# A hybrid attention and SSD encoder layer: 44 of 48 gate and SSD-input tiles multiplied ahead of the heads, in pairs of seven block products

## The reference

```python
h = rmsnorm(x, pre_norm_g)
proj = h @ w_in                                   # 2048 x 13376
q, k, v, z_attn, z_ssm, xbc, dt_raw = split(proj)
o = dilated_attention(q, k, v, rel_bias_table)    # 16 heads x 128
attn_out = rmsnorm(o, attn_norm_g) * silu(z_attn)
ssm_out = ssd_branch(z_ssm, xbc, dt_raw, ...)     # conv 5 + silu, SSD both ways, 32 heads x 64, gate, group rmsnorm
mix = concatenate([attn_out, ssm_out]) @ w_out    # 4096 x 2048
y = x + rmsnorm(mix, post_norm_g)
```

## Time and profile before

| what | value |
|---|---|
| time, median of 3 runs | 2677.62 us (2677.6 to 2677.96) |
| span of the profiled execution | 2675.2 us |
| TensorE busy (matmuls) | 2600.1 us, 97% of the span |
| VectorE, ScalarE busy | 1275.2 us (48%), 791.7 us (30%) |
| matmuls of the input projection (L505) | 10080, of 384 columns |
| DMA | 276.57 MB, mean 103 GB/s |

### The profile page before, as it was taken

The page is one execution under the profiler, slowest core; times in us unless marked ns, Lnnn a source line. Parts: engine busy times, 40 slices in busy tenths (PEclk is TensorE's granted clock), DMA queues, the critical chain, the costliest instruction groups (busy, mean ns, idle before and its releaser), DMA issues.

```text
span 2675.2 us, 37347 instructions
## 1 busy us (share of the span) xinstructions
PE 2600.1 (97%) x14532; PEld 2444.7 (91%) x14532; DVE 1275.2 (48%) x2089; ACT 791.7 (30%) x1259; POOL 0.2 (0%) x4
## 2 busy tenths in 40 slices
PE   6997799999999999999999999999999899999998
PEld 6996799999999999999999999999999788888887
DVE  5544135344453534545343453534445765544447
ACT  5221123323332332323323232332323421111113
POOL 0000000000000000000000000000000000000000
PEclk9998899999999999999999999999999999999999
DMA  4232342432324234232423424243332432222215
GB/s 157 91 111 95 95 127 68 129 121 66 125 64 125 69 124 131 64 122 68 128 78 107 131 60 125 67 129 92 99 122 60 136 132 87 87 87 102 87 64 203
DMA packets 270742, 276.57 MB, mean 103 GB/s; under 512 B 14582, under 2 KB 227766, under 8 KB 266471
## 3 DMA queue, kind: packets, MB, share of 16 engines
q1 hardware_dynamic: 263271, 256.13, 30.4%
q10 hardware_dynamic: 7424, 19.80, 2.0%
HBM read 249.74 MB, written 33.49 MB: 106 GB/s over the span
## 4 chain that ended last, share of the span: by engine, by line
PE 91%; DMA 4%; DVE 1%; SPq 1%; ACT 1%; issue 0%; ACTq 0%; DVEq 0%
PE ps L505 62%; PE ps L711 19%; DMA w_raw<-in_w_in 3%; PE ps L629 2%; PE ps L657 2%; PE ps L596 2%; PE ps L612 1%; SPq L306 1%; PE ps L667 1%; DMA w_raw<-in_w_out 1%; PE ps L634 0%; PE ps L603 0%; PE ps L519 0%; PE ps L720 0%; PE ps L643 0%; PE ps L685 0%
## 5 line engine op out<-in xcount | busy, mean ns | idle before, releaser
L505 PE MATMUL ps<-h_hi,w_hi 128*128 128x384 f32 x3360 | 871.3, 340 | 36.8 <-DVE w_lo L1099 36.4
L505 PE MATMUL ps<-h_lo,w_hi 128*128 128x384 f32 x3360 | 857.7, 336 | 0.0
L505 PE MATMUL ps<-h_hi,w_lo 128*128 128x384 f32 x3360 | 857.5, 336 | 0.0
L1099 DVE TENSOR_TENSOR w_lo<-w_raw,w_hi 128x512 fp32r<-128x512 f32 x420 | 286.7, 690 | 989.3 <-ACT w_hi L788 986.4
L505 PEld LDWEIGHTS ps<-h_hi,w_hi 128*128 128x128 f32 x3360 | 604.9, 189 | 45.8 <-DVE w_lo L1099 25.2
L788 ACT ACTIVATE w_hi<-w_raw 128x512 fp32r<-128x512 f32 x420 | 264.3, 631 | 1260.1 <-PE ps L505 1128.6
L505 PEld LDWEIGHTS ps<-h_hi,w_lo 128*128 128x128 f32 x3360 | 610.5, 189 | 0.0
L505 PEld LDWEIGHTS ps<-h_lo,w_hi 128*128 128x128 f32 x3360 | 610.1, 189 | 0.0
L711 PE MATMUL ps<-h_hi 128*128 128x512 f32 x768 | 299.8, 390 | 0.5 <-issue 0.5
L711 PE MATMUL ps<-h_hi,h_lo 128*128 128x512 f32 x768 | 298.8, 389 | 0.0
L711 PE MATMUL ps<-h_lo,h_hi 128*128 128x512 f32 x768 | 298.8, 389 | 0.0
(11 more groups left out here) (175 smaller groups left out, 1630.5 us busy)
## 6 DMA issues: line engine op xcount, KB each, us to landing
w_raw<-in_w_in SPq DMA_DIRECT2D x416, 256.0 KB, 2.9
stage<-in_w_out SPq DMA_DIRECT2D x30, 1024.0 KB, 5.0
stage<-cb_scr SPq DMA_DIRECT2D x16, 1664.0 KB, 12.7
stage<-loc_scr SPq DMA_DIRECT2D x16, 1536.0 KB, 6.2
stage<-er_scr SPq DMA_DIRECT2D x32, 384.0 KB, 8.8
u_scr<-stage ACTq DMA_DIRECT2D x32, 384.0 KB, 2.5
stage<-u_scr SPq DMA_DIRECT2D x7, 1536.0 KB, 8.0
stage<-in_x_prompt SPq DMA_DIRECT2D x8, 1024.0 KB, 5.6
```

The lines of the kernel that those rows point to most:

```text
L505: last = nc.tensor.matmul(ps[:, 2 * parity + b, 0:HALF_T], w, h[:, k * T + b * HALF_T:k * T + (b + 1) * HALF_T], start=(k == 0 and p == 0) ...
L1099: nc.vector.tensor_tensor(w_lo[:, c, :], w_raw[:, c, :], w_hi[:, c, :].bitcast(f32), ALU.subtract).then_inc(w_lo_done, 1)
```

## The change

The tiles ZA, ZS and XS (48 in all, neighbours in `w_in`) leave the head loop. Four (the first ZA tiles, the "window") are multiplied as before, 16 chunks, in place of iteration 0's. The other 44 are made in 22 pairs ahead of the heads. A pair is a product of a 2x2 block matrix of weights (upper and lower half of the rows, left and right tile) with one of h (upper and lower half of the rows, first and last 384 tokens), by the Winograd form: seven block products in place of eight. A product has two halves of four row blocks, 12 matmuls each: 14 halves, 168 matmuls for two tiles in place of 192. Three sums of h blocks and their splits are kept in `stage` (which the loop uses only later), a fourth takes the place of a block of h, which is stored to `y12_scr` before and loaded back after the pairs. VectorE makes four sums of weights for each pair (`wsum`); ScalarE and VectorE take and add the PSUM results (`snapshot`, `combine`). The raw tiles go to `zx_scr` in DRAM.

The head loop keeps V, Q and K: 12 chunks, one chunk to a step, so each slot follows 24 matmuls in place of 48. Za, zs and xs of a head are loaded from `zx_scr`; ScalarE takes the SiLU in step 3 (`silu_of_gates`). zs is loaded ahead of `reload(a)` and waits for `y_gated` of the head before. The splits of K and Q move to steps 11 and 7, the decay exponents to step 3 and 5. The diff, cut to its core, begins with the constants and SyncE:

```diff
-LOOP_COLS = (COL_V, COL_Q, COL_K, COL_ZA, COL_XS, COL_ZS)
+LOOP_COLS = (COL_V, COL_Q, COL_K)
+WIN = 4
+NP = (GATE_TILES - WIN) // 2
+HP = 14
...
+            def load_z(dst, base, a, done, after, count):
+                src = zx_scr[ds(a * P + base * P, P), :]
+                sp.wait_ge(after, count)
+                sp.dma_start(dst, src).then_inc(done, 16)
...
+            def load_heads(a):
+                load_z(zs, ZX_ZS, a, zs_in, y_gated, a + 1)
+                reload(a)
...
+            for m in range(WIN * NCH):
+                j, c = divmod(m, NCH)
+                load_w(win_chunk(m), COL_ZA + j * P, c)
+                if m % 2 and m + 1 < HEADS:
+                    make_strips(m + 1, strip_out[1])
+                if m == 9:
+                    for q, h in enumerate((h_hi, h_lo)):
+                        sp.dma_start(y12_scr[q * P:(q + 1) * P, :].rearrange("p (k t) -> p k t", k=HK),
+                                     h_block(h, 0, 1).bitcast(f32)).then_inc(y12_out, 16)
...
+            def pair_transfers(p):
+                if not isinstance(p, int) or p > 0:
+                    store_c2(p - 1)
+                load_raw(0, p + 1, wsum_done, 4 * p + 4)
+                load_raw(1, p + 1, w_lo_done, half_of(p, 10))
+                load_raw(2, p + 1, w_lo_done, half_of(p, 12))
+                load_raw(3, p + 1, w_lo_done, half_of(p, 14))
+                store_c1(p)
...
             def iteration(i, a):
                 for m in range(IT_CHUNKS):
                     j, c = divmod(m, NCH)
-                    if m == NCH and a is not None:
-
+                    if m == 1:
+                        load_z(za, ZX_ZA, a, za_in, att_gated, a + 1)
+                    if m == NCH:
                         sp.wait_ge(w_lo_done, chunk_of(i, m) - NCH + 1)
-                        reload(a)
...
+                        load_heads(a)
+                    load_w(chunk_of(i, m), i * P + LOOP_COLS[j], c, waited=(m == NCH))
...
```

On TensorE:

```diff
...
+            def block_half(p, pp, n, bank, hh, hl, start, last):
+
+                pe.wait_ge(w_lo_done, half_of(p, n) + 1)
+                for kk in range(KC):
+                    k = (n % 2) * KC + kk
+                    w_h, w_l = (w[:, n_slot(n, pp), kk * P:(kk + 1) * P] for w in (w_hi, w_lo))
+                    for q, (w, h) in enumerate(((w_h, hh), (w_h, hl), (w_l, hh))):
+                        ins = nc.tensor.matmul(ps[:, bank, 0:HALF_T], w, h(k),
...
+            def pair(p, pp):
...
+                block_product(p, pp, 0, 0, y11, True)
+                if first:
+                    pe.wait_ge(t_lo_done, 1)
+                    pe.wait_ge(tile_out, CONV_TILES)
+                block_product(p, pp, 1, 2, t1, True)
+                pe.wait_ge(snap_done, 3 * p + 1)
+                if first:
+                    pe.wait_ge(t_lo_done, 3)
+                block_product(p, pp, 2, 0, t2, False)
+                block_product(p, pp, 3, 1, y21, True)
+                pe.wait_ge(snap_done, 3 * p + 3)
+                block_product(p, pp, 4, 0, t3, False)
+                block_product(p, pp, 5, 2, y22, False)
+                pe.wait_ge(comb_done, 3 * p + 2)
...
+                block_product(p, pp, 6, 0, t4, False)
...
+            def iteration(i, ip, a):
+                for s in range(IT_CHUNKS):
+                    j, c = divmod(s, NCH)
+                    if a is None and s == 0:
+                        pe.wait_ge(comb_done, 3 * NP)
+                        pe.wait_ge(y12_back, 2)
...
+                    gemm_chunk(chunk_of(i, s), tile_of(i, j), parity_of(ip, j), c)
                     slot(s, a, i)
...
```

On ScalarE:

```diff
...
+            def iteration(i, ip, a, final=False):
+                for s in range(IT_CHUNKS):
+                    m = s + NCH
+                    if not (final and m >= IT_CHUNKS):
+                        split_hi(chunk_of(i, m), m % NCH, tile_of(i, m // NCH))
+                    step(s, a, i, ip)
                     if final and s == 10:
                         silu_of_xs(i)
                         exp_of_decays(i)
...
```

On VectorE:

```diff
...
+            def t_step(s):
+                if s == 4:
...
+                    block_sum(t_block(0), 0, 0)
+                    block_sum(t_block(2), 0, 1)
+                    settle()
+                    nc.vector.tensor_tensor(t_block(0), t_block(2), t_block(0), ALU.subtract).then_inc(t_sum, 1)
...
+                    if n == 3 and first:
+                        dve.wait_ge(tile_done, CONV_TILES)
+                        dve.wait_ge(y12_out, 32)
+                        y21 = h_block(h_lo_f, 0, 1)
+                        block_sum(y21, 1, 0)
+                        settle()
+                        nc.vector.tensor_tensor(y21, y21, t_block(1), ALU.subtract).then_inc(t_sum, 1)
...
+            def iteration(i, ip, a, final=False):
+                for s in range(IT_CHUNKS):
+                    m = s + NCH
+                    if not (final and m >= IT_CHUNKS):
+                        split_lo(chunk_of(i, m), m % NCH)
+                    step(s, a, i, ip)
                     if final and s == 9:
-                        dve.wait_ge(y_gated, i)
+                        dve.wait_ge(y_gated, i + 1)
                         columns_of_channels(i)
                         columns_of_heads(i)
                         settle()
                         convolve_xs(i)
                         decay_exponents(i)
```

More of the change, by code:

```diff
@@ L55 @@
 BROW = 1024
+SBUF_AT = 1152
 RUNS = []
@@ new lines, in _ @@
+            load_raw(1, 0)
+            load_raw(3, 0)
+            sp.wait_ge(rows_stored, 32)
+            sp.wait_ge(cb_stored, 16 * SSM_GROUPS)
+            load_raw(0, 0)
+            sp.wait_ge(win_out[0], 16 * (WIN // 2))
+            load_raw(2, 0)
+            pair_transfers(0)
+            with sp.Fori(1, NP - 1) as p:
+                pair_transfers(p)
+            store_c2(NP - 2)
+            sp.wait_ge(half_done, HTOT - HP + 4)
+            for q in range(2):
+                sp.dma_start(stage[:, 3 * q * HT:(3 * q + 1) * HT], y12_scr[q * P:(q + 1) * P, :]).then_inc(y12_in, 16)
@@ L513, in gemm_half, with gemm_chunk @@
                         last.then_inc(w_used, 1)
+            def gemm_chunk(n, tile, parity, c):
+                if c == 0:
+                    pe.wait_ge(tile_out, tile - 1)
+                pe.wait_ge(w_lo_done, n + 1)
+                for kk in range(KC):
+                    k = c * KC + kk
+                    w_h, w_l = (w[:, c, kk * P:(kk + 1) * P] for w in (w_hi, w_lo))
+                    for p, (w, h) in enumerate(((w_h, h_hi), (w_h, h_lo), (w_l, h_hi))):
+                        for b in range(2):
+                            last = nc.tensor.matmul(
+                                ps[:, 2 * parity + b, 0:HALF_T], w,
+                                h[:, k * T + b * HALF_T:k * T + (b + 1) * HALF_T],
+                                start=(k == 0 and p == 0), stop=(k == KT - 1 and p == 2))
+                last.then_inc(tile_done if c == NCH - 1 else w_used, 1)
             def cb_prompt(g):
@@ L702, in _ @@
-            iteration(0, None)
-            with pe.Fori(0, HEADS - 1) as a:
-                iteration(a + 1, a)
+            for s in range(2 * WIN):
+                j, half = divmod(s, 2)
+                gemm_half(win_chunk(NCH * j), PRO_TILES + j, (1 + j) % 2, half)
+                if s == 0:
+                    cb_prompt(SSM_GROUPS - 1)
+                if s == 1:
+                    cb_sample(SSM_GROUPS - 1)
+                    dt_transposes()
+                if s == 3:
+                    dt_cumulate()
@@ new lines, in of_h, with of_t, block_product @@
+            def of_h(t, kh, th):
+                return lambda k: t[:, (kh * HK + k) * T + th * HALF_T:(kh * HK + k) * T + (th + 1) * HALF_T]
+            def of_t(t, r):
+                return lambda k: t[:, r * HT + k * HALF_T:r * HT + (k + 1) * HALF_T]
+            def block_product(p, pp, q, b, right, start):
+                hh, hl = right
+                for half in range(2):
+                    n = 2 * q + half
+                    block_half(p, pp, n, bank_of(pp, b), hh, hl, start and half == 0, half == 1)
@@ L1370, in step @@
                         convolve_xs(a)
+                if s == 3 and i is not None:
+                    decay_exponents(a)
                 if s == 4:
@@ L1417, in step, with block_sum @@
                     dve.wait_ge(ua_stored, 16 * a + 16)
-            def iteration(i, a, final=False):
-                for s in range(2 * TILES):
-                    for m in (2 * s + 4, 2 * s + 5):
-                        if not (final and m >= IT_CHUNKS):
-                            split_lo(chunk_of(i, m), m % NCH)
-                    if a is None:
-                        dt_step(s)
-                    step(s, a, i)
+            def block_sum(dst, kh, th):
+                did(nc.vector.tensor_tensor(dst, h_block(h_hi, kh, th).bitcast(f32), h_block(h_lo, kh, th).bitcast(f32),
```

(13 more changed lines are left out.)

417 lines of the change are left out of this document (317 added, 100 removed).

## The result

| | before | after |
|---|---|---|
| time, median | 2677.61 us (2677.52 to 2677.96) | 2747.68 us (2744.47 to 2753.18) |
| span of the profiled execution | 2675.2 us | 2742.8 us |
| mean granted clock | 0.988 | 0.968 |
| TensorE, VectorE, ScalarE busy | 97%, 48%, 30% | 93%, 56%, 32% |

The change makes the kernel slower: ratio 1.0263, 95% interval 1.0248 to 1.0277. The span is 67.6 us longer (the median 70.1), though TensorE has 528 matmuls less to do.

A forecast was written before the change was run, and what follows sets the result against it. TensorE was taken as the bound nearly everywhere. Terms -91.7 + 25.1 + 3.4 + 82.7 + 11.2 + 14 = +44.7 gave a span of 2719.9, with 2.4 for the median 2722.3 us; range 2650 to 2765.

The forecast's parts named there:

- A: Likeliest case, head loop: chunk 4's weights behind the reload set each head's pace; 2722 us, bounds 2692 to 2749, chance 0.66.
- the matmuls: Pair stage: 528 matmuls less at an unchanged 173.6 ns each, -91.7 us.
- the way in: Before the pairs: stores of h delay strips, VectorE's sums make TensorE wait; +25.1 us, bounds 12 and 35.
- stall and clock: Head loop: waits for chunk 4's weights, +82.7 us, and slower matmuls from the lowered clock, +11.2.
- L: Head loop: moment in an iteration when chunk 4's weights land, put at 10.1 us; slot 2 can start at L + 11.75.
- B: Rival, head loop: the reload is in time, L under 5.7 us, so faster, 2651 or 2632 us; chance 0.14.
- The point at which the sign turns: Head loop: the landing time L at which slower becomes faster, about 7.7 us with the other terms unchanged.
- the clock: Head loop: stalls may lower TensorE's clock, 0 to 1.6 us a head, middle 0.8 taken, about +11 us.
- The sum by the page: Head loop: at the skill page's 435 GB/s, 4992 KB pass in 11.8 us, L is 4.8, stalls 22.5 in all.
- C: Rival, head loop: VectorE becomes the bound; with 3 us more a head 2764 us; chance 0.13.
- D: Rival, pair stage: halves wait for sums or raw blocks (2744 us at 1 us a pair), or matmuls slow; chance 0.07.
- After the loop: Tail to the main output projection: head 15's decay work and K's split delay its scores; +14 us, bounds 8 and 20.

The follow-up runs named there:

- experiment 1: Changed kernel with the loads of chunk 4 and za issued ahead of zs and the reload: 2664.70 us, ratio to before 0.9951.
- experiment 3: experiment 1 with softmax step 1 on ScalarE and VectorE done before the split of chunk 5: 2648.91 us, ratio 0.9892.
- experiment 4: Changed kernel with the first half of each pair multiplied three times, 528 matmuls more in all: 2836.45 us, ratio 1.0597.
- Experiment 2: Changed kernel with zs loaded behind chunk 4, the reload still ahead of it: 2732.05 us, ratio 1.0203.
- 8: Changed kernel with 16 never-read matmuls of h by h ahead of each head's transposes, to fill the wait: 2754.47 us, ratio 1.0283.
- 9: Changed kernel with 6 never-read plain fp32 matmuls ahead of the transposes in place of the 16 of 8: 2766.12 us, ratio 1.0332.
- experiment 11: 10 with the two stores of h moved into the prologue, the sums left where the change has them: 2637.51 us, ratio 0.9848.
- 10: experiment 3 with K's split ahead of head 15's decay work, and that work and the output weights' split later: 2643.74 us, ratio 0.9872.
- 5: Changed kernel with head 15's decay exponents, exponentials and product with dt moved behind steps 2, 4 and 5 after the loop: 2754.64 us, ratio 1.0282.
- 12: experiment 11 with the work that 10 put behind step 1 after the loop put behind step 2: 2638.28 us, ratio 0.9852.

## Why the prediction was right, and where it was off

Predicted were 2722.3 us, slower, measured 2747.7, in the range of 2650 to 2765 and just inside A's own bounds of 2692 to 2749. Every term but the matmuls came out above its likeliest value, so the sum was short by 22.9 us of span, and the median of the runs lies 3.1 us above the profiled one. One piece of luck is in it: in the way in, a price put too high covers part of a delay that I hadn't seen (below).

**The mechanism (rival A) is shown.** The head's pace is set by chunk 4's weights behind the reload: the circle in the profile after, and experiment 1, which takes the load out of it and gets back 83 us, what I had put down for stall and clock being 93.9. In the two heads shown, whose iterations start at 1420.27 and 1493.01, chunk 4 landed 10.8 and 9.4 us later, where I had L = 10.1. From zs's issue, with which the transfers ahead of chunk 4 begin, to its landing it took 17.8 and 16.4 us, where I had 17.1. The way from the landing to the transposes was 11.7 in both, in place of 11.75, and the transposes came 22.5 and 21.2 us into the iteration, predicted 21.8. All steps of this chain held, since each was read from rows of the same instructions.

**B, faster because the reload is in time,** needed L under 5.7. It was refuted. The point at which the sign turns was given too high: L = 7.7 needs the clock's 11.2 us gone as well; with the other terms as they are it is 10.1 - 44.7 / 14 = 6.9. The sum by the page failed too: the Trainium skill ("DMA: Bandwidth & Descriptors", Specifications) gives a fabric ceiling of 435 GB/s, which made B look likeliest; the trace's stretch 1420 to 1424 us shows

```profile
1420.00:1424.00 4.00, 4.00 (x25) 4.00 (x24) 1.65 (x2) 1.33 (x2) 0.00 (x0) 1.00 1.09 365
```

a DMA share of 1.09 at 365 GB/s. The fabric ceiling was not the price of this transfer. The same table has an HBM limit of about 358 GB/s for a core. By it an estimate for the 4992 KB is 14.3 us, so L = 7.3, and B would not have looked likeliest. The traces agree with neither figure as a mean: 17.8 and 16.4 us here, though one stretch of 4 us before (1058 to 1062) has 399 GB/s.

**C, VectorE as the bound,** did not come: no waits ahead of slots 7 and 9 between 1085 and 2030 us, and experiment 3 brings the period to 66.72 with all of VectorE's work in it. **D** fell with experiment 4 and the 174.0 ns of the chain.

**The head loop's 12.7 us too many** come from two terms, the clock (1.3 us a head, not 0.8) and the transfers, which are not the same in every head. For the clock I had taken the middle between no loss and the loss of the transposes. The trace shows two kinds of head. Among the eleven from 1295.99 to 2026.05, TensorE waits 1.8 to 2.5 us ahead of L754 in one kind; the clock falls there (0.66 from 1433 to 1438 us), and the slow chunk behind it only shortens the next wait (2.2), so it costs nothing. In the other kind the wait ahead of L754 is 1.3 or less and the clock stays up (1.00 from 1358 to 1363 us), the wait ahead of L763 is 3.75 in one piece, and the transposes take 3.67 in place of 1.96 and the chunk behind 4.85 in place of 4.18 (clock 0.50 from 1366 to 1371 us); both are on the path. From the transposes to the end of the next gate it is 43.0 us in the first kind and 45.5 in the second, 44.3 on the mean of 13 heads.

The kind goes with the landing: from the gate's end to it there are 17.4 to 18.1 us ahead of a head of the first kind, 16.5 to 16.9 ahead of one of the second. The 1514.17 - 1442.80 = 71.4 us between the two heads shown have neither loss, the fast clock and the short transfer; I had 71.9 with a transfer between the two. The mean is 73.56. Of the 2.2 between, 1.3 is the slow clock and most of the rest the longer transfer. So per head the stall is about 6.2 (5.8 predicted) and the clock 1.3 (0.8). Experiment 2 agrees: its waits ahead of L754 are short (3.6 us in nine), those of slot 2 are 3.75 in all thirteen heads, and the transposes are slow in all of them. Why the transfers differ from head to head is open, and the clock's price is read from the trace: 8 and 9, which were to test it, didn't isolate it.

**The way in** was 2.6 us dearer. The first matmul of window chunk 14 came at 331.83, where I had 328.3: 10.8 us later than before in place of 7.2. With the stores of h gone from there (experiment 11) it comes at 326.64, so their place costs 5.2, less than my 7.2, and 5.6 us of delay have another cause, which was not looked for. The five sums went nearly as worked out, since 331.1 + 16.8 = 347.9 against the end of the two passes at 347.6. The 2 us for the clock were 1.6: the granted clock is 0.50 from 366 to 369 us, and this is the 0.44 ns x 3648 of the table.

**After the loop** 20 in place of 14. The order of events was right, one row was not: I had the decay rows landing before the convolution's end, and VectorE waited for them (answers to the earlier trace rows; VectorE, ScalarE, TensorE):

```profile
2158.40 3.36 DVE L1509 TENSOR_TENSOR stage<-stage,cur 128x3072 f32<-128x3072 f32 x1 [6.08 <-DMA stage<-loc_scr]
...
2163.58 2.76 ACT L1110 ACTIVATE stage<-stage 128x3072 f32<-128x3072 f32 x1 [8.99 <-DVE stage L1585]
...
2168.13 0.76 PE L747 MATMUL ps<-k_hi,q_hi 128*128 128x512 f32 x1 [13.97 <-issue]
```

The exponents ended at +9.4 after the loop's end (2154.16), predicted +5.7, and the first bias came at 2172.70, +18.5 in place of +13.8. So the first bias is 15.7 us later than before (+2.8), where I had 11.0. Another 3.4 lie between transposes and projection (2181.18 to 2194.63, before 2117.98 to 2128.01), where ScalarE's SiLU stands and I had 2.9. The last 0.9 is in the first pieces of the output projection, where the clock is 0.61 (2194.6 to 2198). That order costs part of this time is shown by 10, which gets back 5.2; 5 failed because I had not asked what stood next on ScalarE, and 12 gained nothing for the same reason.

## What to carry to other kernels

When a stage's tiles are taken out of a loop, list for each transfer what it stands behind and what the loop still has to cover it with; a load of 256 KB behind 4352 KB of zs and reload cost 83 us here, and its place in the list decided the sign. A wait costs more than its length when it is long enough to pull the clock down and the work behind it is on the path. Before moving work out of one wait, look up what comes next on each engine: three of the edits here only met the next item in the list.

## What I had not expected of the hardware

- **A longer loop body on TensorE came with a gap at each return to its start.** With 16 more matmuls in each head, the instruction queue moved 54 packets and 0.89 MB more, 16.5 KB a packet, nine packets for each of the six times that the loop of seven passes goes back to its start, and each time there was a gap of about 4 us, in the one looked at while the data queues were full (DMA share 1.04 at 1350 to 1352 us). That the gap is this fetch is inferred from the counts and the place, not tried by itself. The Trainium skill ("Runtime: NRT & Kernel Launch", Instruction fetch mechanics) says that an engine's instructions come in blocks of 16 KiB through a DMA queue of its own, that TensorE holds 2048 instructions, and that a taken branch out of what it holds must fetch first. The packet size and the place agree; the number 2048 was not tested.
- **The low clock is free in one place and dear in another,** with nearly the same sum of waits: 2.4 and 2.2 us cost nothing, 1.3 and 3.75 cost 2.4 us of slow work, as the head loop's account above shows.
